# Convolution block products as 32-by-32 tiles, and a last value row worked off by token thirds

## The reference, cut to what matters

```python
def causal_dwconv(xp, w, b):
    c = xp.shape[-1]
    y = lax.conv_general_dilated(xp, w[:, None, :].astype(xp.dtype), (1,), 'VALID',
                                 dimension_numbers=('NWC', 'WIO', 'NWC'),
                                 feature_group_count=c)
    return y + b
...
def conv_module(h, buf, w_pw1, b_pw1, w_dw, b_dw, ln_g, ln_b, w_pw2, b_pw2):
    u = h @ w_pw1 + b_pw1
    a, gt = jnp.split(u, 2, axis=-1)
    glu = a * jax.nn.sigmoid(gt)
    xp = jnp.concatenate([buf.astype(glu.dtype), glu], axis=1)
    new_buf = xp[:, xp.shape[1] - (CONV_K - 1):]
    y = causal_dwconv(xp, w_dw, b_dw)
    y = jax.nn.silu(layernorm(y, ln_g, ln_b))
    return y @ w_pw2 + b_pw2, new_buf
```

## Time and profile before

| | |
|---|---|
| time, median of 3 runs | 2660.12 us (2658.79 to 2665.41) |
| the profiled execution: its own time | 2661.12 us |
| its span | 2659.3 us |
| PE busy | 2612.0 us (98%), 18796 matmul records |
| DVE busy | 2185.4 us (82%) |
| POOL busy | 1494.2 us (56%) |
| ACT busy | 963.5 us (36%) |
| block products (L1422) | 1536 records: 39.9 us busy for tiles 1 to 6, 10.2 us for tile 7 |

### The profile page before, as it was taken

The page is one execution under the profiler, slowest core; times in us unless marked ns, Lnnn a source line. Parts: engine busy times, 40 slices in busy tenths (PEclk is TensorE's granted clock), DMA queues, the critical chain, the costliest instruction groups (busy, mean ns, idle before and its releaser), DMA issues.

```text
span 2659.3 us, 46160 instructions
## 1 busy us (share of the span) xinstructions
PE 2612.0 (98%) x18796; PEld 2563.5 (96%) x18796; DVE 2185.4 (82%) x2653; ACT 963.5 (36%) x1593; POOL 1494.2 (56%) x1184
## 2 busy tenths in 40 slices
PE   8999999999999999999999999999999999999998
PEld 8999899999999999999999999989999999999998
DVE  8887778999999898776777777896899999989875
ACT  4012635444444334331222122132444444442433
POOL 4224576777777579762111212127577777765995
PEclk9999999999999999999999999999999999999999
DMA  5333252222111523131111111115322221243231
GB/s 161 66 72 57 100 201 103 70 75 74 69 70 72 215 92 119 54 131 33 42 49 41 49 42 49 41 65 189 137 75 75 75 73 69 74 189 111 84 102 72
DMA packets 162402, 235.08 MB, mean 88 GB/s; under 512 B 77584, under 2 KB 112400, under 8 KB 162192
## 3 DMA queue, kind: packets, MB, share of 16 engines
q1 hardware_dynamic: 81680, 158.36, 17.9%
q10 hardware_dynamic: 80512, 73.78, 8.4%
HBM read 172.91 MB, written 59.20 MB: 87 GB/s over the span
## 4 chain that ended last, share of the span: by engine, by line
PE 91%; DVE 6%; issue 1%; ACT 0%; POOL 0%; DMA 0%; DVEq 0%; ACTq 0%; POOLq 0%
PE BANKS L1283 37%; PE BANKS L1377 13%; PE BANKS L1605 13%; PE BANKS L1243 13%; PE BANKS L1879 3%; PE BANKS L1661 2%; PE BANKS L1422 2%; PE BANKS L1649 1%; PE BANKS L1564 1%; DVE XL L2617 1%; PE BANKS L1716 1%; DVE HGA L3241 1%; PE BANKS L1735 1%; DVE XB_B L3083 1%; PE BANKS L1706 1%
## 5 line engine op out<-in xcount | busy, mean ns | idle before, releaser
L1283 PE MATMUL BANKS<-XB_A,OPS 128*128 128x288 f32 x3432 | 511.2, 297 | 0.0
L1283 PEld LDWEIGHTS BANKS<-XB_A,OPS 128*128 128x128 f32 x3432 | 473.4, 189 | 3.6 <-issue 1.0
L1283 PE MATMUL BANKS<-XB_B,OPS 128*128 128x288 f32 x2904 | 437.2, 296 | 0.0
L998 POOL TENSOR_TENSOR SMALL<-WRAW 128x1 f32<-128x1 f32 x76 | 20.4, 268 | 696.5 <-PE BANKS L1605 455.5
L1283 PEld LDWEIGHTS BANKS<-XB_B,OPS 128*128 128x128 f32 x2904 | 404.1, 189 | 0.0
L3032 DVE SCALAR_TENSOR_TENSOR C<-U,HGA,C 128x1168 f32<-128x1168 f32 x176 | 274.1, 1578 | 36.0 <-ACT C L2283 34.5
L1028 POOL TENSOR_TENSOR OPS<-RAW,OPS 128x512 fp32r<-128x512 f32 x126 | 164.3, 1317 | 200.4 <-ACT OPS L2190 200.4
L1028 POOL TENSOR_TENSOR OPS<-TMP,OPS 128x512 fp32r<-128x512 f32 x168 | 223.2, 1339 | 50.9 <-ACT OPS L2190 50.9
L3104 DVE TENSOR_TENSOR X<-BANKS,X 128x576 f32<-128x576 f32 x224 | 167.8, 750 | 68.0 <-PE BANKS L1377 67.8
L2190 ACT ACTIVATE OPS<-TMP 128x512 fp32r<-128x512 f32 x168 | 106.2, 633 | 283.9 <-POOL TMP L1022 180.6
L1001 POOL TENSOR_TENSOR WL<-WRAW,WH 128x1024 fp32r<-128x1024 f32 x76 | 189.3, 2491 | 6.1
(11 more groups left out here) (368 smaller groups left out, 5981.7 us busy)
## 6 DMA issues: line engine op xcount, KB each, us to landing
RAW<-in_w SPq DMA_DIRECT2D x84, 512.0 KB, 4.2
WRAW<-in_w SPq DMA_DIRECT2D x68, 512.0 KB, 3.6
g_kept<-C ACTq DMA_DIRECT2D x44, 512.0 KB, 2.6
x_kept<-X ACTq DMA_DIRECT2D x24, 576.0 KB, 3.0
XB_BF<-x_kept SPq DMA_DIRECT2D x16, 576.0 KB, 7.8
XB_BF<-g_kept SPq DMA_DIRECT2D x32, 288.0 KB, 4.8
WAY_BF<-g_kept SPq DMA_DIRECT2D x32, 288.0 KB, 4.8
WRAW<-in_w SPq DMA_DIRECT2D x32, 256.0 KB, 3.0
```

The lines of the kernel that those rows point to most:

```text
L1283: ins = nc.tensor.matmul(out[:, cols], w[:, a, p, :], x[:, b, cols], start=s in OPENS and p == 0 and q == 0, stop=p == PAIRS - 1 and q == ...
```

## The change

Each block product becomes one of 32 rows by 32 output columns, so a tile takes 32 x 2 x 4 = 256 products in place of 128, and the four quarters of a group use four different diagonal tiles of the array. The weights no longer hold zeros: `WT` shrinks to 32 x 2 x 32 columns, and all memsets for it and the ScalarE write of zeros go. Tile 7 gets weights, inputs and outputs of its own in the space that this frees (WT_LAST, XT_LAST, BT_LAST); its eight weight transfers are issued on SyncE right behind those of tile 1. The block products of tiles 1, 3, 4 and 5 stand in two parts of 16 groups at steps 0 and 2. V(7) is computed third by third (`last_value`), and VectorE works behind each third (`last_forward`). The products of tile 7 are no longer interleaved with the mean; the mean products of tiles 0 to 5 and of tile 6 follow all of them, between 3 and 4 idle products (before: 6 behind). ScalarE's exponential for the second layer (L2090) moves ahead of `by_blocks(6)`.

```diff
-        WT = WT_FLAT.rearrange("p (g t i) -> p g t i", g=BLK, t=2)
+        WT_F = 2 * BLK * BLK
+        WT, WT_LAST = [WT_FLAT[:, n * WT_F:(n + 1) * WT_F].rearrange("p (g t i) -> p g t i", g=BLK, t=2) for n in range(2)]
...
-                        eng.dma_start(WT[own, :, t, own], taps).then_inc(wt_in, 16)
+                        eng.dma_start(WT[own, :, t, :], taps).then_inc(wt_in, 16)
...
             sp.wait_ge(wp_out, 16)
-            sp.wait_ge(wt_zero, 1)
-
             blocks(sp, TOEPLITZ[0])
+            blocks(sp, KD - 1)
             for u in range(4, U_F0):
-                if u == U_PW2 + 2:
-                    sp.wait_ge(last_zero, 2)
-                    blocks(sp, KD - 1, (2, 3))
                 sp.wait_ge(w_split, u - 1)
                 load(u, u % 2)
...
-            half = 2 * BLK * SW
-            nc.gpsimd.memset(WT_FLAT[:, 0:half], 0.0)
             split(0)
...
-            pool.wait_ge(mb_full, M_N0 + NCH)
-            nc.gpsimd.memset(WT_FLAT[:, half:], 0.0).then_inc(wt_zero, 1)
...
-                if k == 3:
-                    full(pool, pw1_tile("V", KD - 1))
-                    nc.gpsimd.memset(WT_END[:, 0:half], 0.0).then_inc(last_zero, 1)
...
                     for t in range(2):
-                        for own in (slice(0, P // 2), slice(P // 2, P)):
+                        for q in range(0, P, BLK):
+                            own = slice(q, q + BLK)
                             ins = nc.tensor.matmul(PS[own, n % 2 * NCH + g // BANK_GROUPS, at:at + COLS],
-                                                   wt[:, g, t, own], xt[t][:, g, :], start=t == 0, stop=t == 1,
+                                                   wt[own, g, t, :], xt[t][own, g, :], start=t == 0, stop=t == 1,
                                                    skip_group_check=True)
...
-            PARTS = {0: (0, 12), 2: (12, 22), 4: (22, 32)}
+            PARTS = {0: (0, 16), 2: (16, 32)}
...
+            def last_value():
+
+                n, u = pw1_tile("V", KD - 1), U_PW1 + 2 * KD - 1
+                s = u % 2
+                pe.wait_ge(w_split, u + 1)
+                free_slot(n)
+                for c in range(NCH):
+                    for k in range(KD):
+                        wh, wl = WH[:, s, k * P:(k + 1) * P], WL[:, s, k * P:(k + 1) * P]
+                        for q, (w, x) in enumerate(((wh, XH), (wh, XL), (wl, XH))):
+                            ins = nc.tensor.matmul(ps_bank(n, c), w, x[:, k, third(c)],
+                                                   start=(k == 0 and q == 0), stop=(k == KD - 1 and q == 2))
+                    ins.then_inc(value_third if c < NCH - 1 else ps_full, 1)
...
             convolved(KD - 2)
-            for g in range(0, BLK, 4):
-                convolved(KD - 1, g, g + 4)
-                if g == 12:
-                    free_slot(T_MEAN)
-                    for c in range(NCH):
-                        mean(0, c)
-                elif g > BLK // 2:
-                    mean(KD - 2, g // 4 - BLK // 8 - 1)
-            idle_products(6, MB[:, 0, :])
+            convolved(KD - 1)
+            idle_products(3, MB[:, 0, :])
+            free_slot(T_MEAN)
+            for k in (0, KD - 2):
+                for c in range(NCH):
+                    mean(k, c)
+            idle_products(4, MB[:, 0, :])
             for c in range(NCH):
                 mean(KD - 1, c)
...
-            full(act, pw1_tile("V", KD - 1))
-            zeros = IDENT.rearrange("p (a i) -> p a i", a=1).broadcast_to([P, 2 * BLK // 2, P])
-            A(WT_END[:, 2 * BLK * 2 * BLK:].rearrange("p (a i) -> p a i", i=P), zeros, ACT.Identity, scale=0.0
-              ).then_inc(last_zero, 1)
-            act.wait_ge(last_zero, 2)
-            blocks(act, KD - 1, (0, 1))
+            act.wait_ge(lb_in, 1)
+            A(OMLB, LB, ACT.Exp).then_inc(lb_exp, 1)
             by_blocks(6)
...
+            def last_forward():
...
+                for i in range(NCH):
+                    a, b = i * CW, min(SEQ, (i + 1) * CW)
+                    part = glu[:, HIST + a:HIST + b]
+                    if i < NCH - 1:
+                        dve.wait_ge(value_third, i + 1)
+                    else:
+                        full(dve, n)
+                    dc.inc(V.tensor_tensor(part, ps_bank(n, i)[:, 0:b - a], RSTD[:, a:b], ALU.mult))
...
+                    for t in range(2):
+                        b0, b1 = done[t], SEQ // BLK if i == NCH - 1 else b // BLK - t
+                        rows = glu[:, (b0 + t) * BLK:(b1 + t) * BLK].rearrange("p (b j) -> p b j", j=BLK)[:, :, ::-1]
+                        ins = V.transpose(by_block[t][:, b0:b1, :], rows)
...
-            glu_of(7)
-            forward(7)
+            last_forward()
             back(6)
```

66 lines of the change are left out of this document (47 added, 19 removed).

## The result

| | before | after |
|---|---|---|
| median of the runs | 2659.45 us (4 runs, 2658.64 to 2665.41) | 2690.56 us (4 runs, 2690.38 to 2694.31) |
| profiled execution, span | 2661.12 us, 2659.3 us | 2694.31 us, 2692.5 us |
| granted clock, mean of the span | 0.996 | 0.987 |
| matmul records | 18796 | 20334 |

The changed kernel is slower: ratio 1.0115, 95% interval 1.0098 to 1.0133, 31 us. The forecast was 2639 us with a range up to 2662, so it lies 52 us off and on the other side. The profiled execution was 3.8 us above the median of its runs; up to the centring, which is what the document is about, it is 30.0 us behind the profile before (310.81 against 280.81 us).

A forecast was written before the change was run, and what follows sets the result against it. TensorE was taken as the bound (91% of the chain). Rows -11.0, last tiles -11.3 and SyncE's queue +0.5 us gave -21.8 us from the profiled 2661.12: 2639 us, range 2631 to 2662.

The forecast's parts named there:

- The record's length: Block products: r, the time per small record, taken as 10 ns with four tiles at once, from 8.4 to 14.7.
- Rival (a): Block products: only two array tiles work at a time, r = 17 ns, 2660 us; chance 0.15.
- rival (c): Block products: tiles of different rows writing the same PSUM bank take turns, r = 34 ns, 2712 us; chance 0.06.
- 0.512 r + 0.6 us: Block products of one tile: 512 records of r ns in two bursts, 5.7 us at 10 ns instead of 8.47.
- Rival (b): Block products: records can't start oftener than today, r stays 29.4 ns with twice the records, 2698 us; chance 0.13.
- The rows' term: Block products of tiles 1, 3, 4, 5: from 8.47 to 5.7 us each, -11.0 us in all.
- The last tiles: Tile 6's first product to tile 7's mean product: 17.8 us instead of 29.15, TensorE never stopping, -11.3 us.
- Rival (d): Tiles 6 and 7: a quarter-filled array may lose the 2.4 GHz clock, 3 to 5 us more, 2643 us; no separate chance.
- SyncE's queue: Eight more transfers ahead of the fifth weight load make GpSimd's split 0 to 2.2 us late: 0 to +1.0, taken +0.5 us.
- GpSimd's and ScalarE's freed work: Dropped memsets (3.5 us) and one write of zeros: hidden before or part of the wait already counted, no further gain.
- The last value row by thirds: V(7): same 72 products and weight loads, so no cost; VectorE works behind the first thirds, tile 7's inputs come in time.

The follow-up runs named there:

- run 4: Changed kernel with half the block products, each twice as wide under the first group's weights, so the second group's weights are missing from the result: 2644.97 us.
- run 11: Kernel before with small products in the rows only, in four parts of 8 groups, plus nine idle products between tile 6's and tile 7's block products: 2653.16 us.
- run 3: Changed kernel with mean products again among tile 7's groups of four and six idle products after the last: 2685.74 us.
- run 2: Changed kernel with tile 7's eight transfers issued on SyncE behind weight load 7, not ahead of weight load 4: 2684.78 us.
- run 8: Changed kernel without its last value row by thirds, VectorE's gating and transposes behind the whole row as before: 2689.90 us.
- runs 10 to 12: Kernel before, small products in rows only, four parts of 8 groups: 2652.14 us; plus idle products: 2653.16; changed kernel, that layout, tile 7's transfers later: 2658.91.

## Why the prediction was wrong, point by point

**The record's length was right.** The forecast took 10 ns with 8.4 as the lower bound; the rows show 9.6 to 9.8 where records flow, and 80 columns take 18.4. Rival (a) (17 ns, two tiles at a time) and rival (c) (34 ns, tiles of different rows take turns at one PSUM bank) are refuted. By the Trainium skill, "TensorEngine Tiling (Array Packing)", section "Gotcha 1: PSUM Pressure", different row tiles cannot write the same bank at once; here four of them write one bank on different partitions 9.7 ns apart on average, where 34 would be in turn. The Trainium skill's floor of about 25 ns between starts ("TensorE: Matmul & The Clock Gate", section "Wait — 56ns, not 53.3ns?") isn't seen either, since over 200 records in a row average 9.7 ns. The measurement decides in both.

**The step that failed is the one from the record to the row**: "0.512 r + 0.6 us". It took a burst to be its records and nothing else. The change triples the rate at which TensorE consumes instructions, and the prediction said so ("as the instructions come three times as dense as now") but drew only a margin on r from it. Rival (b) named "instructions coming in" as one reason among three and made of it a longer distance between all starts, 29.4 ns; in truth the price comes in lumps, about 2 us per 256 instructions in a row, and none at all where there is room between them. From tile 3's burst to tile 4's: 5.6 us of products; 1.91 + 0.38 + 2.09 = 4.4 us of pauses; and 2.0 us by which the two rows exceed their 24.96, some 1.5 for the lower clock behind the pauses (23.61 us against 22.07 in run 4), the rest for the changes. Products and changes come to 6.1 us, forecast were 5.7. The rows' term was to be -11.0 us and was +15.5.

**The last tiles**: forecast 17.8 us, measured 37.5. "TensorE never stops, the clock has no idle stretch before it" is the sentence that failed. The old idle stretch did go: tile 7 was ready 3.4 us behind its value row, and nobody waited for a transfer. Seven pauses came in its place, 12.2 us together, and with TensorE idle for almost half of the time the clock is at its lower level for most of it (0.57). So 128 records take 2.35 us there, 1.0 more than at full clock, but as the pauses are shorter the price is half of that: 4.0 us from pause to pause, where it was 3.5 at full clock (94.95 to 98.41 us). Rival (d) had the lower clock, with 3 to 5 us, but as an effect of a quarter-filled array. The run with wide products, as small a part of the array, ran at 0.99 from 243 to 257 us, so it is not that. The idling is what is left, and run 11 shows that filling an idle stretch keeps the clock up. The means and idle products behind the blocks took another 8.4 us (forecast 7.3) that could stand in the pauses; 4.8 us came back when they did (run 3).

**SyncE's queue**: forecast +0.5 us with +1.0 as the upper bound, measured +5.8 by run 2 and +6.1 in the profile. Sizes were off. Sixteen issues took 16.8 us, not twice 6.31, so the load was issued at 61.8, not 58.0; the first eight alone took 8.9 us (8.8 in run 2), and why these are longer than before the runs don't show. The load landed in 4.8 us, not 6.6, and GpSimd's split took 4.4, not 3.65. And the price of TensorE's waiting was left out: after 5.4 us idle the row took 14.82 us for 12.48. The range said "2.2 us late" for a late landing; it was 5.1.

**GpSimd's and ScalarE's freed work** shows nowhere in the 30.0 us, as forecast; no run took it alone. **The last value row by thirds** was worth nothing (run 8), against the forecast: it was to remove a stop, and the pauses made it unneeded.

**The chances.** With the supply and the queue wrong and the record's length right, the true case was a mixture of (b) and (d) that had no number among the rivals. What the profile before did show was how dense the instructions had been at most: 29.4 ns a record with its weight load, 15 ns an instruction, 3.8 us for a packet of 256. The changed kernel's tiles 6 and 7 go at 4.0 us a packet (276.75 to 300.67 in six). The page lists the instruction packets; dividing the one by the other could have given (b) its right shape: what comes in is whole packets, and nothing in the trace showed that they come faster than one in 3.8 us. That was reason for more than 0.13.

## What to carry to other kernels

Splitting a product into smaller ones that run side by side pays in busy time, but each small one still has to be fetched: count the instructions in a row, not only their time. Here parts of up to 128 records (256 instructions) with 3.3 us of large products between them left pauses for instructions of 0.3 to 1.1 us, and not at every part (runs 10 to 12); 256 records in a row cost about 2 us of standing and then up to half the clock behind it. A burst of small transfers put ahead of a load delays the load by its own issue (7.9 us here), and of that reaches the time what the load had no room for, with the clock's fall where TensorE waits: 5.8 us.
